# Two attentions worked in pairs of heads, the stick-breaking one between the second halves of the q, k and v projections

## The reference, cut to what matters

```python
def attn_hybrid_mixer(h, w_qkv, w_o, pos):
    qkv = (h @ w_qkv).reshape(B, S, 3, N_ATT_HEADS, HEAD_DIM).transpose(2, 0, 3, 1, 4)
    q, k, v = qkv[0], qkv[1], qkv[2]
    sb = stick_breaking_attention(q[:, :N_SB_HEADS], k[:, :N_SB_HEADS], v[:, :N_SB_HEADS])
    mb = moba_attention(rotary(q[:, N_SB_HEADS:], pos), rotary(k[:, N_SB_HEADS:], pos), v[:, N_SB_HEADS:])
    o = jnp.concatenate([sb, mb], axis=1).transpose(0, 2, 1, 3).reshape(B, S, ATT_W)
    return o @ w_o
# stick-breaking, one block of queries
    z = jnp.einsum('bhqd,bhkd->bhqk', qb, k) * scale
    log_1mb = jnp.where(strict, jax.nn.log_sigmoid(-z), 0.0)
    after = lax.cumsum(log_1mb, axis=3, reverse=True) - log_1mb
    a = jnp.where(strict, jnp.exp(jax.nn.log_sigmoid(z) + after), 0.0)
# modulation of a layer, from the conditioning vector c
    m = jax.nn.silu(c) @ w + b      # 1024 x 6144 for each of the two layers
```

## Time and profile before

| | us |
|---|---|
| median of three runs | 2444.39 (2443.2 to 2445.96) |
| the profiled execution | 2445.56, span 2443.8 |
| projections q, k, v in it (1514.3 to 1585.0) | 70.7 |
| rotation (to 1594.9) | 9.9 |
| eight stick-breaking heads (to 1660.4) | 65.5 |
| eight softmax heads, split, gate's rows (to 1750.5) | 90.1 |
| output projection, residual, norm, to the first matmul of the feed-forward (to 1785.1) | 34.6 |

### The profile page before, as it was taken

The page is one execution under the profiler, slowest core; times in us unless marked ns, Lnnn a source line. Parts: engine busy times, 40 slices in busy tenths (PEclk is TensorE's granted clock), DMA queues, the critical chain, the costliest instruction groups (busy, mean ns, idle before and its releaser), DMA issues.

```text
span 2443.8 us, 30335 instructions
## 1 busy us (share of the span) xinstructions
PE 2162.1 (88%) x12462; PEld 1444.5 (59%) x12462; DVE 1070.2 (44%) x1591; ACT 700.4 (29%) x875; POOL 77.6 (3%) x50
## 2 busy tenths in 40 slices
PE   7988899989988888888888885977789989958998
PEld 7988897843333333333333323943589878947996
DVE  6996756332222222222222226332455546355554
ACT  4433454411111111111111112362333334423332
POOL 0242110000000000000000000000000000000000
PEclk9989999979999999999999997975789989979999
DMA  9434567579999999999999995563345535404552
GB/s 314 174 121 164 181 218 282 206 287 420 418 418 418 418 418 418 417 418 418 417 418 417 418 412 207 183 230 138 104 138 173 190 138 204 176 0 149 183 185 78
DMA packets 222602, 652.75 MB, mean 267 GB/s; under 512 B 6672, under 2 KB 70160, under 8 KB 189360
## 3 DMA queue, kind: packets, MB, share of 16 engines
q1 hardware_dynamic: 222512, 651.44, 69.4%
HBM read 650.37 MB, written 1.05 MB: 267 GB/s over the span
## 4 chain that ended last, share of the span: by engine, by line
PE 53%; DMA 31%; DVE 10%; ACT 3%; issue 2%; POOL 0%; SPq 0%; DVEq 0%; ACTq 0%; POOLq 0%
DMA ring<-w_down 30%; PE bank L672 25%; PE bank L692 12%; PE bank L928 5%; DVE arena L1606 2%; PE bank L902 2%; DVE ring_low L1556 2%; PE bank L735 2%; PE bank L743 1%; ACT w_high L1152 1%; PE bank L978 1%; PE bank L704 0%; PE bank L713 0%; DVE arena L1620 0%; PE bank L884 0%
## 5 line engine op out<-in xcount | busy, mean ns | idle before, releaser
L1556 DVE TENSOR_TENSOR ring_low<-ring,w_high 128x2048 fp32r<-128x2048 f32 x180 | 412.5, 2295 | 387.4 <-ACT w_high L1152 386.1
L672 PE MATMUL bank<-x_high,w_high 128*128 128x256 f32 x1728 | 500.1, 289 | 40.6 <-DVE ring_low L1556 27.9
L672 PE MATMUL bank<-x_low,w_high 128*128 128x256 f32 x1728 | 496.9, 288 | 0.0
L672 PE MATMUL bank<-x_high,ring_low 128*128 128x256 f32 x1728 | 496.4, 287 | 0.0
L902 PE MATMUL bank<-ring,arena 128*64 128x512 f32 x2048 | 458.0, 595 | 30.7 <-DMA ring<-w_gu 29.7
L1152 ACT ACTIVATE w_high<-ring 128x2048 fp32r<-128x2048 f32 x180 | 339.7, 1891 | 235.5 <-PE bank L692 129.3
L672 PEld LDWEIGHTS bank<-x_high,w_high 128*128 128x128 f32 x1728 | 340.0, 197 | 44.6 <-issue 29.9
L1894 DVE TENSOR_TENSOR arena<-bank,par 128x512 f32<-128x512 f32 x64 | 44.0, 687 | 687.5 <-PE bank L911 687.5
L902 PEld LDWEIGHTS bank<-ring,arena 128*64 128x64 f32 x2048 | 141.7, 136 | 336.8 <-issue 256.1
L672 PEld LDWEIGHTS bank<-x_low,w_high 128*128 128x128 f32 x1728 | 340.0, 197 | 0.6 <-issue 0.5
L672 PEld LDWEIGHTS bank<-x_high,ring_low 128*128 128x128 f32 x1728 | 339.7, 197 | 0.0
(11 more groups left out here) (273 smaller groups left out, 2093.1 us busy)
## 6 DMA issues: line engine op xcount, KB each, us to landing
ring<-w_gu SPq DMA_DIRECT2D x128, 2048.0 KB, 24.6
ring<-w_down SPq DMA_DIRECT2D x64, 2048.0 KB, 26.1
ring<-ada_w SPq DMA_DIRECT2D x24, 2048.0 KB, 8.0
ring<-ffn_w_gate_up SPq DMA_DIRECT2D x44, 1024.0 KB, 7.3
ring<-ret_w_in SPq DMA_DIRECT2D x12, 2048.0 KB, 7.8
ring<-w_in SPq DMA_DIRECT2D x10, 2048.0 KB, 7.8
ring<-w_in SPq DMA_DIRECT2D x16, 1024.0 KB, 10.1
ring<-ffn_w_down SPq DMA_DIRECT2D x8, 2048.0 KB, 7.6
```

What stands on the lines that cost most here:

```text
L672: mm = pe.matmul(acc_bank[:, ch * T:(ch + 1) * T], w[:, k, ch * P:(ch + 1) * P], xs[:, kk, :], start=kk + ch + n == 0, stop=kk == b.kc - 1 ...
L1556: V.tensor_tensor(low_part(u), raw_part(u), high_part(u).bitcast(F32), ALU.subtract).then_inc(sem("w_low"), 1)
```

## The change

The order of the weights changes, and with it the order on PE, ACT and DVE.

- The tiles now come as first half of q, of k, of v, modulation tile 12, second half of q, tile 13, second half of k, tile 14, second half of v, then tiles 15 to 21, first half of the output projection, 22, its second half, 23. The first halves hold the eight stick-breaking heads.
- Two PSUM banks make one `pair` of 1024 columns, and one instruction on ACT or DVE works on two heads (128x768 instead of 128x384). All four pairs keep their own buffers (`a_z`, `a_e`), and a stage is done for all four before the next: scores, Exp, Ln, sum over later keys, Exp, output. The copy of the scores, the negated absolute value and the rectified value change engine or form: one Copy on ACT, two operations on DVE instead of Abs and Relu on ACT.
- On PE the stick-breaking stages stand between the units of the second halves, with products 12 to 14 and reductions 12 to 14; the rotation too.
- The softmax heads follow in four pairs, with two score stages ahead and products 15 to 20 between; products and reductions 21 to 23 follow one after another behind the last head, ahead of the gate's rows.
- Each modulation tile is reduced in its own bank and added by DVE at once (`ada_in`); PE no longer waits for the second layer's modulation ahead of the output projection.
- The outputs of two pairs share a bank and are copied by ACT (before: DVE).

The diff, cut to its core:

```diff
+        aq.append(plan.block([(qkv_w, 0, 512)]))
+        ak.append(plan.block([(qkv_w, D, 512)]))
+        av.append(plan.block([(qkv_w, 2 * D, 512)], token=True))
+        plan_ada()
+        aq.append(plan.block([(qkv_w, 512, 512)]))
+        plan_ada()
+        ak.append(plan.block([(qkv_w, D + 512, 512)]))
...
+        plan_ada()
+        a_outs += plan_groups(1)
+        av.append(plan.block([(qkv_w, 2 * D + 512, 512)], token=True))
...
         plan.stop()
-        ada_tiles(12)
-        ao = [plan.block([(a["att_w_o_2"][0], 512 * i, 512)], token=True) for i in range(2)]
+        for _ in range(3):
+            plan_ada()
...
+        ada_tiles(1)
+        ao = [plan.block([(a["att_w_o_2"][0], 0, 512)], token=True)]
+        ada_tiles(1)
+        ao.append(plan.block([(a["att_w_o_2"][0], 512, 512)], token=True))
+        ada_tiles(1)
...
+            def sb_scores(p):
+                wait_evac(pe, aq[0].groups[p // 2])
+                wait_evac(pe, ak[0].groups[p // 2])
+                if p >= 2:
+                    pe.wait_ge(sem("a_zs"), p - 1)
+                for j in range(2):
+                    r = head_rows(j)
+                    pe.matmul(heads2[p % 2][:, j, 0:T], kk2[r, p, 0:P], q2[r, p, :], start=True, stop=True)
+                for j in range(2):
+                    r = head_rows(j)
+                    mm = pe.matmul(heads2[p % 2][:, j, T:T + P], kk2[r, p, P:T], q2[r, p, P:T], start=True, stop=True)
+                mm.then_inc(sem("a_z"), 1)
...
+                    pe.wait_ge(sem("a_t"), p - 1)
+                for j in range(2):
+                    dst, L = heads2[p % 2][:, j, :], a_e[p][:, j, :]
+                    pe.matmul(dst[:, 0:T], k1("later"), L[:, 0:T], start=True, stop=False)
+                    pe.matmul(dst[:, P:T], ones[:, :], L[:, T:T + P], start=False, stop=True)
+                    mm = pe.matmul(dst[:, T:T + P], k1("later"), L[:, T:T + P], start=True, stop=True)
+                mm.then_inc(sem("a_after"), 1)
...
+                for j in range(2):
+                    r = head_rows(j)
+                    pe.matmul(heads2[0][:, j, 0:P], q2[r, 4 + m, 0:P], kk2[r, 4 + m, 0:P], start=True, stop=True)
+                for j in range(2):
+                    r = head_rows(j)
+                    mm = pe.matmul(heads2[0][:, j, P:P + T], q2[r, 4 + m, P:T], kk2[r, 4 + m, :], start=True, stop=True)
+                mm.then_inc(sem("b_s"), 1)
...
+            feature(aq[0], s_h[0])
+            feature(ak[0], s_h[0])
+            sb_scores(0)
+            sb_scores(1)
+            token(av[0], s_h[0], units=(0,))
+            sb_scores(2)
+            sb_scores(3)
+            token(av[0], s_h[0], units=(1,))
+            ada_product(12)
+            feature(aq[1], s_h[0], units=(0,))
...
-            for i in range(NSB + 2):
-                if i < NSB:
-                    r, c = head_rows(i)
-                    if i >= 2:
-                        pe.wait_ge(sem("a_L"), i - 1)
-                    b = bank[4 + i % 2]
-                    pe.matmul(b[:, 0:T], kk2[r, c, 0:P], q2[r, c, :], start=True, stop=True)
-                    pe.matmul(b[:, T:T + P], kk2[r, c, P:T], q2[r, c, P:T], start=True,
-                              stop=True).then_inc(sem("a_z"), 1)
-                if 1 <= i <= NSB:
-                    h = i - 1
-                    pe.wait_ge(sem("a_L"), h + 1)
...
-                    L = a_L[h % 2]
...
-                if 1 <= i <= 6:
-                    ada_reduce(11 + i)
-                if i < 6:
-                    ada_product(12 + i)
...
+            sb_after(0)
+            sb_after(1)
+            ada_reduce(12)
+            feature(aq[1], s_h[0], units=(1,))
+            sb_after(2)
+            sb_after(3)
+            ada_product(13)
+            feature(ak[1], s_h[0], units=(0,))
+            sb_out(0)
+            sb_out(1)
+            ada_reduce(13)
+            rope_swap(0)
+            rope_swap(1)
+            feature(ak[1], s_h[0], units=(1,))
+            ada_product(14)
+            sb_out(2)
+            sb_out(3)
+            token(av[1], s_h[0], units=(0,))
+            ada_reduce(14)
+            rope_swap(2)
+            rope_swap(3)
+            token(av[1], s_h[0], units=(1,))
+            ada_product(15)
+            soft_scores(0)
+            ada_reduce(15)
+            ada_product(16)
+            soft_scores(1)
+            soft_turn(0)
+            soft_scores(2)
+            ada_reduce(16)
+            ada_product(17)
+            soft_turn(1)
+            soft_out(0)
+            soft_scores(3)
+            ada_reduce(17)
+            ada_product(18)
+            soft_turn(2)
+            soft_out(1)
+            ada_reduce(18)
+            ada_product(19)
+            soft_turn(3)
+            soft_out(2)
+            ada_reduce(19)
+            ada_product(20)
+            soft_out(3)
+            ada_reduce(20)
+            for i in range(21, 24):
+                ada_product(i)
+                ada_reduce(i)
             split_ready("attn2")
             gate_rows(0)
...
-                    link(nc.scalar.activation(a_e[i % 2], z, ACT.Abs))
-                    link(nc.scalar.activation(a_e[i % 2], a_e[i % 2], ACT.Exp, scale=-HD ** -0.5))
-                    link(nc.scalar.activation(a_e[i % 2], a_e[i % 2], ACT.Ln, bias=1.0))
-                    nc.scalar.activation(a_r[i % 2], z, ACT.Relu, scale=HD ** -0.5).then_inc(sem("a_sp"), 1)
-                if i >= 1:
-                    h = i - 1
-                    act.wait_ge(sem("a_t"), h + 1)
-                    if h >= 2:
-                        act.wait_ge(sem("a_o"), h - 1)
-                    nc.scalar.activation(a_A[h % 2], a_t[h % 2], ACT.Exp).then_inc(sem("a_exp"), 1)
...
+            copy_features(aq[:1], q2)
+            copy_features(ak[:1], kk2)
+            sb_copy(0)
+            sb_copy(1)
+            high_until(units_of(aq[1])[0])
+            sb_exp(0)
+            sb_exp(1)
+            sb_copy(2)
+            sb_copy(3)
+            high_until(units_of(aq[1])[1])
+            sb_exp(2)
+            sb_exp(3)
+            copy_tokens(av[:1], v2)
+            for p in range(NSB // 2):
+                sb_ln(p)
+            ada_take(12)
...
+            sb_weights(0)
+            sb_weights(1)
+            copy_group(aq[1].groups[1], q2[:, 6:8, :].rearrange("p c t -> p (c t)"))
+            sb_weights(2)
+            sb_weights(3)
...
+            sb_in(1)
+            copy_tokens(av[1:], v2[:, :, 512:1024])
+            ada_take(15)
+            soft_exp(0)
+            ada_take(16)
+            for g in a_outs:
+                wait_evac(act, g)
+            split_high("attn2", which=(0,))
+            soft_exp(1)
...
+            split_high("attn2", which=(1,))
+            ada_take(21)
             high_until(units_of(ao[0])[1])
-            act.wait_ge(sem("b_oT"), NSB // 2)
-            split_high("attn2")
+            ada_take(22)
+            ada_take(23)
...
+            def sb_logs(p):
+                dve.wait_ge(sem("a_ln"), p + 1)
+                link(V.scalar_tensor_tensor(out=a_e[p], in0=a_z[p], scalar=0.0, in1=a_e[p], op0=ALU.max, op1=ALU.add))
+                link(V.tensor_tensor(a_z[p], a_z[p], a_e[p], ALU.subtract))
+                V.tensor_tensor(diag(a_e[p]), diag(a_e[p]), masks("strict"), ALU.mult).then_inc(sem("a_L"), 1)
...
+                V.tensor_copy(soft[k][:, :, P:T], heads2[0][:, :, P:T])
+                V.tensor_tensor(diag(soft[k]), diag(heads2[0]), masks("causal"), ALU.add).then_inc(sem("b_masked"), 1)
+                dve.wait_ge(sem("b_masked"), m + 1)
+                V.tensor_reduce(bmax[k][:, 0:2], soft[k][:, :, 0:P], AX_X, ALU.max)
+                link(V.tensor_reduce(bmax[k][:, 2:4], soft[k][:, :, P:P + T], AX_X, ALU.max))
+                V.tensor_scalar(bneg[k], bmax[k], -HD ** -0.5, None, ALU.mult).then_inc(sem("b_max"), 1)
...
+            low_until(units_of(av[0])[0])
+            dve.wait_ge(sem("c2_in"), 32)
...
+            for p in range(NSB // 2):
+                sb_logs(p)
+            low_until(units_of(ak[1])[0])
+            sb_less(0)
+            sb_less(1)
+            sb_mask(0)
+            sb_mask(1)
+            low_until(units_of(ak[1])[1])
+            ada_in(12)
+            sb_less(2)
+            sb_less(3)
+            sb_mask(2)
...
+            soft_mask(0)
+            ada_in(15)
+            soft_mask(1)
+            soft_scale(0)
+            split_low("attn2", (0,))
+            soft_mask(2)
...
+            for i in range(18, 21):
+                ada_in(i)
+            split_low("attn2", (1,))
+            for i in range(21, 24):
+                ada_in(i)
...
-            modulation(1)
-            split_low("attn2")
             gate_diags(0, 0, 2, "attn2")
             low_until(units_of(ao[0])[1])
+            modulation(1)
```

395 lines of the change are left out of this document (218 added, 177 removed).

## The result

| | before | after |
|---|---|---|
| median of four runs, us | 2443.87 (2443.2 to 2445.96) | 2366.67 (2365.12 to 2370.31) |
| span of the profiled execution | 2443.8 | 2363.3 |
| mean granted clock | 0.94 | 0.961 |

The ratio is 0.9685, with a 95% interval of 0.9668 to 0.9702: 3.2% faster, 77 us instead of the forecast 54.

What follows compares the result with a forecast made beforehand. PE was taken to bound the projections and heads, then clock and waits the softmax stage: 104 + 68 + 5 = 177 us instead of 236.2. So 2445.6 - 59 + 4.3 = 2390.9, less 1.2: 2390 us; range 2373 to 2411.

Steps and rivals of the forecast that it cites:

- Stage A: Projections with stick-breaking heads between them, from 1514.3 us to the end of v: bound by PE at full clock, 104 us.
- rivals 3 and 4: 3: PE held at first stage's joints, 2400 to 2412, chance 0.16; 4: half clock for projections too, 2480, chance 0.03.
- The order at k's second half: Tightest place of the projection stage: k's second tile ready at 60 us, PE wants it at 67.
- The late feed-forward tile: Behind the output projection: first feed-forward tile waits for a ring slot, delaying DVE's adds, norm and feed-forward by 4.3 us.
- The step for the gate's rows: Between last reduction and output projection: DVE's diagonals and four full-width matmul passes at half clock, about 5 us.
- the term of the heads: PE's stick-breaking work: eight heads x (0.91 + 1.08 + 0.79) = 22.2 us, less 3.9 for pairs.
- The discount for side by side: Scores and outputs of a pair's two heads on PE: 29% less, 3.9 us; bounds 0% and 50%.
- The 3 us that I added for hand-overs: Projection stage: allowance of 3 us for hand-overs between some 20 small steps.
- Stage B: Softmax heads to last reduction: 68 us, between 52 at full clock and 77 at half clock.
- the clock step: Softmax stage's PE clock put two thirds of the way to half: 52 + 0.67 x 25, 68 us.
- Rival 1: Softmax stage at the full clock: 52 us, 2374 us in all; chance 0.18.
- The laying out of DVE and ACT: Softmax stage at full clock: DVE and ACT, taking turns within pairs, end last, at about 52 us.

Runs made afterwards that it cites:

- e4_ring: Changed kernel with modulation tiles 21 to 23 loaded ahead of both output projection tiles, and ACT's high parts of these behind its takes; 2352.56 us.
- e6_apart: Changed kernel with stick-breaking scores and outputs issued for all even heads, then all odd ones, two pairs at a time; 2369.56 us.
- e2_gap: Changed kernel with twelve needless DVE copies in the second softmax pair's mask, lengthening PE's wait at the softmax stage's head; 2376.43 us.
- e3_small: Changed kernel with modulation tiles 15 to 23 loaded to a quarter (256 of 1024 rows), same instructions on PE, ACT and DVE; 2358.67 us.
- e7_fill: On top of e4_ring, each modulation product from tile 17 on issued one step earlier, filling PE's wait ahead of the first softmax transposes; 2352.78 us.

## Why the prediction was off, step by step

**What held.** Stage A is PE's: it is busy 96.93 of 98.40 us at 0.97, against 0.96 in the projections before; rivals 3 and 4 did not come. Three table loads are left. The order at k's second half held. 70.7 + 8.5 for products and reductions + 3.6 for swaps + 13.1 for heads make 95.9, and the stage took 98.4. The late feed-forward tile cost 3.9 of the forecast 4.3, by the path named (low parts ahead of the adds), and e4_ring gave it back. The step for the gate's rows (5) measured 4.8.

**Stage A, 104 against 98.4: the term of the heads was too big.** "Eight heads x (0.91 + 1.08 + 0.79)" less 29% made 18.3 us; measured are 4 x 0.76 + 8 x 0.88 + 4 x 0.75 = 13.1. The discount for side by side, from one row at half clock, was of the right size after all: 3.9 us, against 3.2 by e6_apart. What failed is the price of one head. It was read where each step stands between others, and the new order issues four heads' steps in a row, which cost less than four alone: 5.4 us, told above as 18 hand-overs of 0.3, for which the sum had nothing. (The 0.91 instead of 0.84 was 0.5 more.) The 3 us that I added for hand-overs stand beside 2.5 in the measurement, of which 1.5 are idle PE. The Trainium skill (TensorEngine Tiling (Array Packing), Key Properties and Theoretical Speedup) gives up to twice for tiles of 64. Here two pairs cost 39% less side by side than apart for scores (1.51 against 2.47) and 31% less for outputs (1.50 against 2.16), 1.6 and 1.4 times as fast, or 1.8 and 1.6 by an estimate that takes the hand-over out of both; all of it is within that bound. The row of before, with its 29%, was a fair one for outputs.

**Stage B, 68 against 53.0: the clock step failed.** The step was "I put it two thirds of the way to half clock", 16 us of the forecast (52 + 0.67 x 25 is 68.7, which I wrote as 68). In after, the clock of B is 0.90. I took the 20.00 busy us at 0.50 as a property of this mix of small steps, but e2_gap shows stage B's work back at the full clock 8 us behind a wait of 9. What I should have read is what PE did before the clock fell: a wait of 2.66 us ahead of those 20 us, and 2.61 us ahead of the transposes of seven of the eight softmax heads (the 19.4 us of the earlier trace rows), each time with half clock behind it. Stage B has one such wait, and the late tile. The Trainium skill (TensorE: Matmul & The Clock Gate, What's actually happening) says that a busy PE is released to 2.4 GHz. After and e2_gap agree with it, 4 and 8 us behind the wait. The 20 busy us at 0.50 of before don't, unless the release may take that long, and no run here tells.

Rival 1 (B at the full clock, 52 us, 2374 in all) is what happened, but for the half clock behind two waits; it had a chance of 0.18. The argument against it, the 4 us gap at the head, was worth 4 us of half clock and no more. That its 52 us is close to 53.0 is luck: two errors cancel. The laying out of DVE and ACT was 7.5 us too long, as e4_ring's 44.5 shows. And I had costed nothing for the transfers: I moved tile 23 behind the second tile of the output projection in the ring, followed that move to the feed-forward only, and did not ask when tile 23 itself would land once B is short. Its product waited 6.61 us and ran at half clock after that; e3_small (8 us) and e4_ring (8.5) price it.

**In sum:** from the stage's start to the feed-forward, -5.6 in stage A, -15.0 in B, -0.2 for the gate's rows and -0.4 in the tail make 21.2 of the 23 us between the forecast and the measured median. The range ended at rival 1 with stage A as forecast. It did not combine rival 1 with a stage A below the forecast, which its own bound for pairs (50%, 3 us) already asked for.

## What to carry to other kernels

Price a small PE step from two rows, one where it stands alone and one where several follow each other, and count how often the new order changes from one kind to another. When a stretch shows half clock, look first at PE's waits ahead of it. In this part of the ten traces PE was at half clock at once or within 3 us behind every wait of 2.4 us or more, and mostly, not always, kept the full clock over waits of 0.7 to 1.2; small steps without longer waits kept it. And when a stage gets shorter, go through the queue of transfers once more, with the new times: a tile that is needed last in a stage must not stand behind one that is needed only in the next.

## What the runs showed of the hardware

- Scores of a head (two fp32 products on 64 rows of the array) cost 0.84 us alone, 0.62 in a row of four heads of which neighbours mostly use the same 64 rows (e6_apart), and 0.38 when neighbours use the other 64 (after); outputs on 64 columns 0.79, 0.54 and 0.38. A pair's scores between other steps cost 0.86, as much as one head's.
- Behind a wait the clock came back to 2.4 GHz after 4, 8, 13.3 or 23.8 us with PE nearly always busy, in kernels that differ little, and the longest time did not follow the longest wait (waits of 3.52, 9.02, 3.84 and 2.66 us). I expected one number.
- The same wait of 1.13 us ahead of the gate's rows left them at the full clock in e4_ring (1.96 us) and at half in e7_fill (3.40 us) and after (3.65 us).
- Up to the stage the same instructions took 1512.0 to 1515.2 us in ten profiled executions, so a shift of 3 us at a position in the middle of a trace means nothing unless it is taken from the stage's own start.
